# A hybrid MoBA and gated DeltaNet layer on one Trainium2 core: 16-bit halves handled by GpSimd, softmax weights turned by DMA, two head chains shifted by two slots

## What is computed

```python
h = rms_norm(x, norm_gain)
aq, ak, av, az, bqkv, bz, bbeta, balpha, gate_a, gate_b = jnp.split(h @ w_in, cuts, axis=-1)
ya = moba_attention(to_heads(aq), to_heads(ak), to_heads(av)) * jax.nn.silu(az)
bqkv = short_conv(bqkv, conv_w)                      # 4 taps, causal, then SiLU
o = gated_delta_rule(bq, bk, bv, g, beta)            # chunked, a triangular solve in it
yb = rms_norm(o, dn_norm_gain) * jax.nn.silu(to_heads(bz))
merged = (jax.nn.sigmoid(gate_a) * (ya @ w_branch_a)
          + jax.nn.sigmoid(gate_b) * (yb @ w_branch_b))
x = rms_norm(x + merged @ w_out, final_norm_gain)
```

## Time and profile before

| | us |
|---|---|
| three runs | 788.03, 789.00, 789.43 |
| median | 789.0 |
| the profiled execution | 788.17 |
| its span in the trace | 786.4 |
| PE busy | 764.7 (97%) |
| DVE busy | 553.3 (70%) |
| ACT busy | 467.6 (59%) |
| POOL busy | 102.1 (13%) |
| DMA, share of 16 engines | 72% |

### The profile page before, as it was taken

The page is one execution under the profiler, slowest core; times in us unless marked ns, Lnnn a source line. Parts: engine busy times, 40 slices in busy tenths (PEclk is TensorE's granted clock), DMA queues, the critical chain, the costliest instruction groups (busy, mean ns, idle before and its releaser), DMA issues.

```text
span 786.4 us, 10433 instructions
## 1 busy us (share of the span) xinstructions
PE 764.7 (97%) x3507; PEld 627.6 (80%) x3507; DVE 553.3 (70%) x1265; ACT 467.6 (59%) x697; POOL 102.1 (13%) x167
## 2 busy tenths in 40 slices
PE   8998999999999999999999999999999999999996
PEld 6887887888788878878887788788778888888884
DVE  5779748965895698479658956884797566765563
ACT  5686557656764766477567556764765764435440
POOL 5112010110101020101101010111020100001120
PEclk9999999999999999999999999999999999999999
DMA  9968757876687778668766877687676576688652
GB/s 250 247 169 199 201 161 188 220 193 173 184 221 198 177 194 209 174 177 219 193 172 179 214 207 172 180 206 201 172 193 199 176 197 189 181 264 272 192 160 108
DMA packets 219333, 152.89 MB, mean 194 GB/s; under 512 B 49168, under 2 KB 184336, under 8 KB 219152
## 3 DMA queue, kind: packets, MB, share of 16 engines
q1 hardware_dynamic: 219136, 151.96, 71.6%
q10 hardware_dynamic: 144, 0.26, 0.1%
HBM read 140.64 MB, written 2.11 MB: 182 GB/s over the span
## 4 chain that ended last, share of the span: by engine, by line
PE 67%; DMA 9%; ACT 8%; DVE 7%; SPq 5%; issue 4%; DVEq 0%; POOLq 0%; POOL 0%; ACTq 0%
PE pj L602 20%; PE pj L600 20%; PE pj L601 20%; DMA turned<-halves 9%; SPq L334 3%; DVE w_lo L1146 3%; ACT w_hi L865 2%; ACT moT L916 1%; ACT convs L935 1%; SPq L298 1%; ACT L947 1%; DVE kk L1299 1%; ACT yT L916 1%; PE pj L851 1%; PE pj L849 1%
## 5 line engine op out<-in xcount | busy, mean ns | idle before, releaser
L1146 DVE TENSOR_TENSOR w_lo<-w_raw,w_hi 128x1024 fp32r<-128x1024 f32 x251 | 307.5, 1230 | 157.3 <-ACT w_hi L865 155.9
L600 PE MATMUL pj<-w_hi,xt_hi 128*128 128x512 f32 x860 | 345.9, 402 | 0.4 <-DVE w_lo L1146 0.4
L602 PE MATMUL pj<-w_hi,xt_lo 128*128 128x512 f32 x860 | 336.6, 391 | 0.0
L601 PE MATMUL pj<-w_lo,xt_hi 128*128 128x512 f32 x860 | 335.9, 391 | 0.0
L865 ACT ACTIVATE w_hi<-w_raw 128x1024 fp32r<-128x1024 f32 x251 | 263.5, 1054 | 118.4 <-PE pj L602 106.6
L602 PEld LDWEIGHTS pj<-w_hi,xt_lo 128*128 128x128 f32 x860 | 161.4, 188 | 34.3
L600 PEld LDWEIGHTS pj<-w_hi,xt_hi 128*128 128x128 f32 x860 | 161.8, 188 | 32.2 <-issue 0.6
L601 PEld LDWEIGHTS pj<-w_lo,xt_hi 128*128 128x128 f32 x860 | 161.9, 188 | 31.1
L1333 DVE SCALAR_TENSOR_TENSOR xs<-lrep,xs 128x31 f32<-128x31 f32 (+30 forms) x496 | 80.0, 231 | 0.0
L535 POOL TENSOR_TENSOR xo<-v,own 128x128 f32<-128x128 f32 x16 | 14.7, 919 | 125.3 <-DVE v L1342 87.3
L1273 DVE SCALAR_TENSOR_TENSOR conv<-kk,hs,conv 128x255 f32<-128x255 f32 (+2 forms) x72 | 29.7, 475 | 0.0
(11 more groups left out here) (292 smaller groups left out, 734.6 us busy)
## 6 DMA issues: line engine op xcount, KB each, us to landing
w_raw<-in_w_in_dram SPq DMA_DIRECT2D x384, 256.0 KB, 3.4
w_raw<-in_w_out_dram SPq DMA_DIRECT2D x64, 256.0 KB, 3.7
w_raw<-in_w_branch_a_dram SPq DMA_DIRECT2D x32, 256.0 KB, 3.6
w_raw<-in_w_branch_b_dram SPq DMA_DIRECT2D x32, 256.0 KB, 3.7
gate<-in_x_dram SPq DMA_DIRECT2D x8, 256.0 KB, 5.3
gate<-in_x_dram SPq DMA_DIRECT2D x4, 512.0 KB, 7.1
gate<-in_final_norm_gain_dram SPq DMA_DIRECT2D x1, 1024.0 KB, 9.4
out_dram<-gate SPq DMA_DIRECT2D x4, 256.0 KB, 3.5
```

Source lines behind the costliest of these rows:

```text
L600: pe.matmul(bank[:, t, :], hi[:, k, tok], w_hi[:, slot, cs], start=(k == 0), stop=False)
L601: pe.matmul(bank[:, t, :], hi[:, k, tok], w_lo[:, slot, cs], start=False, stop=False)
L602: mm = pe.matmul(bank[:, t, :], lo[:, k, tok], w_hi[:, slot, cs], start=False, stop=(k == kt_all - 1))
L1146: dve.tensor_tensor(w_lo[:, slot, :], w_raw[:, slot, :], w_hi[:, slot, :].bitcast(F32), ALU.subtract).then_inc(lo_ready, 1)
```

## The change

1. All laying apart and joining of 16-bit halves moves from ACT to POOL, into `head`: `dn_nat` (two copies), the three joins of `u`, `mo_nat` (two), the join of `moT`, the laying apart and joining of both outputs. The steps `S_HALVES`, `S_JOIN`, `M_HALVES`, `M_JOIN`, `M_YA` go; ACT keeps the two SiLU steps that stood with them, at `S_Z` 20 and `M_Z` 36.
2. The softmax weights go through halves and a transposing DMA as well (`turn_p`, behind unit `J_P` 2 of the next head), and POOL joins them into `probT`. The three PE transposes of a head and ACT's copy from PSUM go.
3. The DeltaNet chain from the convolution on stands two slots earlier (`S_TURN` 20, `S_CONV` 22, `S_SILU` 24, `S_KK` 26, `S_BACK` 38, `SUB` 31 to 43, up to `S_O` 63).
4. The scores stand two slots later (`M_QK` 40, `M_EXP` 42) and the product with the values six later (`M_PV` 50, `M_YT` 56), in the next head's turn.
5. Since the last head's MoBA output now comes later, phase A takes its units in another order, `A_ORDER`: three units of chunk 0, three of chunk 1, then the last of each. `gate_a` of a chunk follows two units behind the chunk's last unit.
6. `half_squared` becomes further counts of `f_total`.

```diff
+A_ORDER = [(0, 0), (0, 1), (0, 2), (1, 0), (1, 1), (1, 2), (0, 3), (1, 3)] + [(c, j) for c in (2, 3) for j in range(4)]
+A_LAST = [max(n for n, (at, _) in enumerate(A_ORDER) if at == c) for c in range(NC)]
-S_NAT, S_HALVES, S_DEC, S_JOIN, S_TURN, S_CONV, S_SILU, S_KK, S_BACK = 15, 17, 18, 21, 22, 24, 26, 28, 42
-J_YA, J_DN, J_YB, J_MO, J_BACK = 5, 14, 16, 22, 23
+S_NAT, S_DEC, S_TURN, S_Z, S_CONV, S_SILU, S_KK, S_BACK = 15, 18, 20, 20, 22, 24, 26, 38
+J_P, J_YA, J_DN, J_YB, J_BACK, J_MO = 2, 6, 14, 15, 20, 21
-M_NAT, M_HALVES, M_JOIN, M_QK, M_EXP, M_PT, M_PV, M_YA, M_YT = 31, 33, 37, 38, 40, 42, 44, 46, 51
+M_NAT, M_Z, M_QK, M_EXP, M_PV, M_YT = 31, 36, 40, 42, 50, 56
...
+            def turn_p(h):
+                sp.wait_ge(p_halves_ready, h + 1)
+                sp.dma_start_transpose(turned[:, 0:6, :], p_halves).then_inc(p_landed, 16)
...
+                for t in range(T):
+                    pool.wait_ge(dn_nat_ready, T * h + t + 1)
+                    pool.tensor_copy(dn_halves[:, :, :, t, :],
+                                     dn_nat[:, t, 0:3 * P].bitcast(U16).rearrange("p (a n e) -> p a e n", a=3, e=2)
+                                     ).then_inc(dn_halves_ready, 1)
                 if not first:
                     output_norm(h - 1)
+                    yb_apart(h - 1)
+                    pool.wait_ge(o_done, h)
+                pool.wait_ge(dn_landed, 16 * h + 16)
+                for a in range(3):
+                    joined(u[:, a, :], dn_halvesT[:, 4 * a:4 * a + 4, :].rearrange("p (e t) n -> p e (t n)", e=2), u_ready)
...
+                pool.wait_ge(prob_ready, T * h + T)
+                pool.tensor_copy(p_halves.rearrange("p (e n) -> p e n", e=2), apart(prob[:, :])).then_inc(p_halves_ready, 1)
...
-                if s == M_PT:
-                    pe.wait_ge(prob_ready, T * h + T)
-                    for i in range(3):
-                        mm = pe.transpose(C[:, i * P:(i + 1) * P], prob[:, i * P:(i + 1) * P], ident[:, :])
-                    mm.then_inc(pt_done, 1)
...
-                    if c > 0 and j == 1:
-                        gate_a(c - 1)
+                if n - 2 in A_LAST:
+                    gate_a(A_LAST.index(n - 2))
```

More of the change, by code:

```diff
@@ L366, in chunk, with load @@
                 for j in range(units):
[L367 to L375, removed]
-                    if wmat is w_b and c * units + j == J_YB - UNITS * 2 // 3:
-                        sp.wait_ge(yb_halves, H)
-                        turn_y(yb_landed)
-            for c in range(NC):
-                chunk(w_a, c, BU, FIRST_A)
+                    load(wmat, col, j, c * units + (first_unit + j))
+            def load(wmat, col, j, number):
+                sp.wait_ge(lo_ready, number - RING + 1)
+                for i in reversed(range(UK)):
+                    k = UK * j + i
+                    sp.dma_start(w_raw[:, number % RING, i * CH:(i + 1) * CH],
+                                 wmat[k * P:(k + 1) * P, col:col + CH]).then_inc(w_landed[number % RING], 16)
+            for n, (c, j) in enumerate(A_ORDER):
+                load(w_a, c * CH, j, FIRST_A + n)
+                if n == J_P:
+                    turn_p(H - 1)
+                if n == J_YA:
+                    sp.wait_ge(ya_halves, H)
+                    turn_y(ya_landed)
+                if n == J_YB:
+                    sp.wait_ge(yb_halves, H)
+                    turn_y(yb_landed)
             for c in range(0, NC):
@@ new lines, in head @@
+                pool.wait_ge(v_ready, (LEVELS + 1) * h + 1)
+                pool.tensor_tensor(xo[:, :], v[:, :], own[:, 0, :], ALU.mult).then_inc(xo_ready, 1)
+                if not first:
+                    pool.wait_ge(pv_done, h)
+                pool.wait_ge(p_landed, 16 * h + 16)
+                joined(probT[:, :], turned[:, 0:6, :].rearrange("p (e b) n -> p e (b n)", e=2), pt_ready)
+                pool.wait_ge(ya_ready, T * h + T)
+                pool.tensor_copy(halves[:, 0, :].rearrange("p (e n) -> p e n", e=2),
+                                 apart(ya[:, :, :].rearrange("p t n -> p (t n)"))).then_inc(ya_halves, 1)
@@ L536, in head @@
+                pool.wait_ge(v_ready, (LEVELS + 1) * h + 2)
+                pool.tensor_tensor(xo[:, :], v[:, :], own[:, 1, :], ALU.mult).then_inc(xo_ready, 1)
+                if not first:
+                    pool.wait_ge(yb_lo_ready, h)
+                pool.wait_ge(ya_landed, 16 * h + 16)
+                joined_y(yaT_ready)
                 pool.wait_ge(v_ready, (LEVELS + 1) * (h + 1))
@@ L552, in _ @@
             output_norm(H - 1)
+            yb_apart(H - 1)
+            yb_joined(H - 1)
             pool.wait_ge(gain_landed, 16)
```

181 lines of the change are left out of this document (80 added, 101 removed).

## The result

The changed kernel takes 841.43 us (median of 4 runs, 840.26 to 844.16); the kernel before, on the same chip, 788.51 (787.78 to 789.43). The ratio is 1.0675, with a 95% interval of 1.0646 to 1.0704. It is slower by 53 us, where 22 had been forecast. The profiled execution spans 838.5 us, 52.1 more than that of before, and that difference is what has to be accounted for.

A forecast was written before the change was run, and what follows sets the result against it. PE, busy for 97% of the span, was taken as the bound, with DVE second from the convolution to SUB's end. 788.2 + 16.1 (seven heads) + 1.2 (head 0) + 4.8 (phase A) = 810.3, as median 811 us; range 782 to 823.

The forecast's parts named there:

- Blocking: POOL's copies hold DVE up for up to their whole length: 1.1 us in the convolution, 5.4 together in SUB's ledger.
- Rivals C and D: C: POOL's copies block DVE half as much, 786 us, chance 0.13; D: they don't block, 779 us, chance 0.12.
- S_KK: At the S_KK products PE waits 2.0 us a head for convs, bounds 0 and 3, instead of 0.68.
- Scores and transposes: At M_QK the wait for moT, 1.08 us a head, goes; so do PE's softmax-weight transposes, 0.24 us.
- Phase A: Ahead of unit 8 PE stands still once for gate_a of chunk 0: 4.8 us, bounds 3 and 5.5.
- The stretch of SUB: During SUB PE waits for w_lo of unit 25: 2.3 us a head, bounds 0 and 3.5.
- The ledger: Sum for w_lo's lead in SUB: 4.2 + 0.4 + 0.65 - 5.4 - 1.5 - 0.6 = -2.3 us a head.
- Head 0: The first head, without a previous output, loses 1.2 us, against 2.3 in each of the others.
- rival A: The forecast itself: POOL's copies block DVE in full, 803 to 819 us, chance 0.45.

The follow-up runs named there:

- The pair of copies and memsets: Kernel before with three unused POOL copies of 768 halves a head behind the join of q and v: 795.18 us; with memsets instead: 787.00 us.

## Why the prediction was wrong

**Blocking: right as a whole, less so in its parts.** It was put at 1.1 us in the convolution and 4.3 in the stretch of SUB a head; DVE's busy time rose by 5.8, of which 1.6 in the convolution, 3.0 in the steps of SUB and 1.2 in `w_lo`, 15 of which take 1.6 to 1.9 us. Rivals C and D are ruled out. The pair of copies and memsets shows the cause for the steps of SUB; for the convolution it is read from what lies beside it.

**S_KK: right.** 2.0 us a head were forecast; the products cost 3.16 us a head against the 1.09 of the earlier trace rows without a wait, so 2.07. That it goes when the chain is put back shows that the slots make it; how much of `convs`' lateness is blocking was not tested by itself.

**Scores and transposes: right.** Both disappear from PE. The products at M_QK cost 0.47 us a head, so 1.17 was won there for the 1.08 forecast, and the 0.24 of the earlier trace rows are gone.

**Phase A: right.** 4.8 us were forecast; the stop is 4.6, and one turn earlier takes 3.6 of it away. The slow clock behind it was not in the forecast.

**The stretch of SUB: the step that failed.** The ledger took the lead of `w_lo` of unit 25, 4.2 us, as what DVE's lateness would use up first. But PE meets `xe` ahead of that `w_lo`, and there the reserve was much smaller. In head 4 of before, S_KK starts at 348.41, `xe` ends at 378.73 and PE starts S_Y at 379.25 without having waited:

```profile
378.41 0.32 DVE L1237 TENSOR_TENSOR xe<-vt,own 128x128 f32<-128x128 f32 x1
...
379.25 0.39 PE L654 MATMUL dn_ps<-xe,mt 128*128 128x128 f32 x2
```

From S_KK on that is 30.3 us for DVE and 30.8 for PE. After, `xe` is 32.85 behind S_KK (403.78 - 370.93), and PE would be ready 29.4 behind it (400.31 - 370.93). DVE lost 2.5, and PE came 1.4 sooner, since it no longer waited at M_QK, had no transposes and had M_PV behind S_Y. The 0.5 in between was all there was in this head; in the others it is 0.9 (0.8 of it of use), with DVE losing 2.6 and PE 1.5 sooner. So PE stops for 3.4 us where 2.3 were forecast at `w_lo`, which hardly waits any more because the stop at `xe` gives it time. Over eight heads the first S_Y costs 27.9 us more (29.1 for 1.2), where some 18 had been forecast for `w_lo`. I had listed "SUB's last group with `v` and `xe` comes ahead of this `w_lo`" as a cost to `w_lo` without asking who waits for `xe`.

**Head 0.** 1.2 us were forecast; here DVE waits 3.3 us for POOL's join of `kk` with the next `w_lo` behind it in its list, and PE stops for 3.1 us on that `w_lo`.

**The clock: missing altogether.** 16.4 us, a third of the loss. The forecast put it at nothing without a word. In the trace of before the clock is at full speed and the longest stop within the heads is 2.1 us, so it gave neither the size of this term nor its absence; I had not asked what the four to five microseconds forecast for phase A, or stops that come with every head, do to the clock.

With +35.7 for the waits and less 2.0, the time would have been 788.5 + 33.7 = 822: above the 803 to 819 of rival A, and just inside 823, the top of the range. The clock took it outside. Of the 30 us between the forecast 811 and the measured 841, 16.4 are the clock and 9.5 the stop at the first S_Y, which was put in the wrong place and too short.

## What to carry to other kernels

Work moved to an idle GpSimd isn't free if it reads SBUF while DVE, the second bound, works through instructions that read SBUF too. As an upper bound, count each such copy's whole duration as DVE time; here the rows beside a copy lost 1.0 to 1.4 us, and the fourteen copies of a head 5.8 us. Then ask at every place where PE meets DVE's results, not only at the one that seems to set the pace, how much reserve there is. When a stop of TensorE appears that repeats in every iteration, allow besides its length for a slow clock behind it (here up to 1.7 us each time), and take a small step towards the change (here two slots for the scores, one for S_KK, which gave 0.8%) before the large one.
